# Half of the tokens' merge, output, norm and query moved beside the other half's experts

## The reference

```python
h = rmsnorm(x, g1) * (1 + sc1) + sh1
p = h @ w_in                                    # attention, short convolution, long convolution, gates
g_att, g_sc, g_hy = split(sigmoid(p[..., GT0:]), 3)
m = g_att * (y_att @ w_att) + g_sc * (y_sc @ w_sc) + g_hy * (y_hy @ w_hy)
x = x + gt1 * (m @ w_o)                         # the merge and the output projection
h2 = rmsnorm(x, g2) * (1 + sc2) + sh2
# experts: for each token 8 heads, each with the 16 best of 128*128 experts
q = h2 @ wq;  s = q . subkeys;  e, score = top 16 of the sums of the top 16 of both halves
a = gelu(u_tab[e] . h2);  f = sum over heads and experts of softmax(score) * a * v_tab[e]
x = x + gt2 * f
```

## Time and profile before

| | us |
|---|---|
| median of three runs | 5394.02 |
| lowest, highest | 5386.65, 5394.62 |
| span of the profiled execution (first to last instruction) | 5406.6 |
| busy in it: PE matmul | 3763.2 (70%) |
| PE weight load | 1823.9 (34%) |
| VectorE | 3264.4 (60%) |
| ScalarE | 1947.0 (36%) |
| GpSimd | 1959.6 (36%) |
| DMA, all queues | 1532.43 MB, mean 283 GB/s |

### The profile page before, as it was taken

How to read it: one execution, slowest core, us unless ns; L and a number is a source line. 1 busy time by engine, 2 the same in 40 slices (tenths; PEclk the granted TensorE clock), 3 DMA queues, 4 the chain that set the end, 5 groups by cost and what they waited for, 6 DMA issues and landing times. The chain is left out here.

```text
span 5406.6 us, 59650 instructions
## 1 busy us (share of the span) xinstructions
PE 3763.2 (70%) x19504; PEld 1823.9 (34%) x19504; DVE 3264.4 (60%) x7012; ACT 1947.0 (36%) x5112; POOL 1959.6 (36%) x1521
## 2 busy tenths in 40 slices
PE   6899879987555555555497788668976555555554
PEld 3677338876111111111122245246852111111111
DVE  7522452323777777777647778764136777777776
ACT  5432002222434334434334434325223433443443
POOL 5112003322444444444343356212433444444443
PEclk7999889998777777777798889889987777777777
DMA  5011001112999999999999989831328999999998
GB/s 238 16 44 71 4 16 63 62 71 89 399 420 410 414 408 421 413 414 415 391 407 358 361 335 378 348 146 42 100 84 334 421 410 416 410 418 416 410 418 347
DMA packets 230644, 1532.43 MB, mean 283 GB/s; under 512 B 26164, under 2 KB 26740, under 8 KB 58044
## 3 DMA queue, kind: packets, MB, share of 16 engines
q0 software_dynamic: 184320, 1342.26, 60.7%
q1 hardware_dynamic: 46012, 186.36, 9.3%
HBM read 1515.31 MB, written 13.21 MB: 283 GB/s over the span
## 5 line engine op out<-in xcount | busy, mean ns | idle before, releaser
L536 PE MATMUL psum<-arena 64*64 64x512 f32 x10240 | 1752.8, 818 | 1230.9 <-ACT arena L515 1207.1
L491 POOL DMA_INDIRECT arena<-in_uv,arena x1280 | 1446.9, 1130 | 1878.1 <-PE psum L536 1438.7
L651 DVE SCALAR_TENSOR_TENSOR arena<-arena 128x1024 f32<-128x1024 f32 x1280 | 1597.5, 1248 | 736.9 <-DMA arena<-in_uv,arena 681.0
L536 PEld LDWEIGHTS psum<-arena 64*64 64x64 f32 x10240 | 415.4, 168 | 2524.9 <-ACT arena L515 1880.4
L1527 PE MATMUL psum<-view_at,view_at 128*128 128x512 f32 (+1 forms) x4896 | 964.7, 358 | 19.3 <-PEq L165 10.3
L504 ACT ACTIVATE arena<-arena 128x1 f32<-128x1 f32 x1280 | 258.3, 202 | 1865.1 <-DVE arena L651 1794.2
L1527 PEld LDWEIGHTS psum<-view_at,view_at 128*128 128x128 f32 x4896 | 813.9, 191 | 183.7 <-issue 53.3
L265 POOL TENSOR_TENSOR view_at<-view_at,view_at 128x1024 fp32r<-128x1024 f32 (+1 forms) x180 | 398.8, 2225 | 1208.7 <-ACT view_at L299 1207.7
L515 ACT ACTIVATE arena<-arena 128x64 f32<-128x64 f32 x1280 | 445.1, 348 | 75.8 <-PE psum L536 33.9
L508 ACT ACTIVATE arena<-arena 128x1 f32<-128x1 f32 x1280 | 376.8, 294 | 47.1 <-ACT arena L504 0.8
L299 ACT ACTIVATE view_at<-view_at 128x1024 fp32r<-128x1024 f32 (+1 forms) x176 | 164.0, 939 | 327.9 <-DMA view_at<-in_w_in 186.4
(11 more groups left out here) (243 smaller groups left out, 3368.4 us busy)
## 6 DMA issues: line engine op xcount, KB each, us to landing
view_at<-in_w_in SPq DMA_DIRECT2D x108, 512.0 KB, 5.6
view_at<-in_w_mod SPq DMA_DIRECT2D x48, 1024.0 KB, 11.6
arena<-in_uv,arena POOLq DMA_INDIRECT x1280
view_at<-in_w_br SPq DMA_DIRECT2D x48, 256.0 KB
view_at<-in_w_out SPq DMA_DIRECT2D x16, 512.0 KB, 8.7
view_at<-in_wq SPq DMA_DIRECT2D x16, 512.0 KB, 3.3
arena<-mod_rows SPq DMA_DIRECT2D x12, 512.0 KB
keep_spectrum<-arena SPq DMA_DIRECT2D x18, 256.0 KB, 7.3
```

The costliest lines, as they stand in the source:

```text
L491: nc.gpsimd.indirect_dma_start(out=self.slots[i % self.ring], out_offset=None, in_=self.table, in_offset=bass.IndirectOffsetOnAxis(ap=self ...
L536: last = nc.tensor.matmul(self.c.psum[tokens, at:at + 512], self.diag[rows, k % 4], self.slots[k % self.ring][rows, D + h * 512:D + (h + 1 ...
L651: nc.vector.scalar_tensor_tensor(out=self.junk, in0=self.slots[i % self.ring][:, 0:D], scalar=1.0, in1=self.h2_turned if i % 2 else self.h ...
```

## The change

Layer 1: merge, out, norm2 and query run on the four latent tiles only. The context's rounded input h and its three branch outputs are stored to DRAM at the start of the merge. The experts then run alone for 260 steps (the phase is given 260, two tiles and 4). The context pair's merge, output, norm and query follow as one phase, `phase_later_beside`, beside the steps 260 to 492, and the experts go on alone to step 520.

Layer 2: the same with the second pair of latent tiles; its phase runs beside the steps 0 to 236 of the first pair.

`phase_later_beside` has a list of steps with weights: a lead, 24 gates and 24 values, the eight blocks of `w_out`, the norm, the eight blocks of `wq`, each 256 tokens wide. All weights are loaded from DRAM a second time, through a ring of three slots that lie where space is left (`ScatteredRing`). The sigmoid is written with tanh, `(tanh(z/2) + 1) * v`, and m is halved when it is rounded. It uses the PSUM banks 0 to 3, so the experts' tiles beside it are on banks 4 to 7: `(4, 0, 4, 0, 4, 4)` becomes `(4, 0, 4, 4, 4, 4)` and `(0, 4, 0, 4)` becomes `(4, 4, 0, 4)`.

```diff
 class Share:
-    def __init__(self, experts=None, first=0, last=0, steps=1):
-        self.experts, self.first, self.n, self.steps = experts, first, last - first, steps
+    def __init__(self, experts=None, first=0, last=0, steps=1, weights=None):
+        self.experts, self.first, self.n = experts, first, last - first
+        self.ends = [0] + list(itertools.accumulate(weights or [1] * steps))
...
+LAST_LATENTS = Later(2, 0, 152, (88, 96), 168, ((176, 180), (189, 193), (197, 132)))
+CONTEXT = Later(4, 1, 168, (96, 80), 136, ((144, 148), (189, 193), (197, 132)))
...
+def later_steps():
+    steps, weights = [("lead", i) for i in range(3)], [4] * 3
+    for g in range(N_GATES):
+        steps += [("gate", 2 * g), ("value", 2 * g + 1)]
+        weights += [4, 2]
+    steps += [("merged", i) for i in range(2)]
+    weights += [1] * 2
+    steps += [("out", N_MERGE + b) for b in range(KD)]
+    weights += [4] * KD
+    steps += [("added", i) for i in range(2)] + [("norm", i) for i in range(6)]
+    weights += [1] * 2 + [2] * 6
+    steps += [("query", N_MERGE + KD + h) for h in range(PH)]
+    weights += [5] * PH
+    steps += [("scored", i) for i in range(2)]
+    weights += [1] * 2
+    return steps, weights
...
+def phase_later_beside(c, layer, where, experts, first, last, h_kept, ys_kept):
...
+        @ph.block.gpsimd
+        def _(pool):
+            for s, (kind, n) in enumerate(steps):
+                share.gpsimd(pool, s)
+                if kind == "lead" and n == 2:
+                    ring.split(pool, 0)
+                if kind in ("gate", "value", "out", "query"):
+                    ring.split(pool, n + 1)
...
+                    feature_job(c, ring.parts(n), bank(n), W, kt, of, after=lambda k: share.tensor(pe, s, k, kt)).then_inc(proj, 1)
...
+                    nc.scalar.activation(sig[:, g % 2], c.psum[:, bank(n - 1):bank(n - 1) + W], ACT.Tanh, scale=0.5).then_inc(sig_d, 1)
...
+                if kind in ("gate", "value", "out", "query"):
+                    ring.round_one(act, n + 2)
...
 def phase_merge
+            ring.load(sp, proj, range(SLOTS))
+            for dst, src in stores:
+                sp.dma_start(dst, src).then_inc(stored, 16)
+            ring.load(sp, proj, range(SLOTS, n_all))
...
 def build
-        phase_merge(c, 0, lay)
-        phase_out(c, 0, True, lay)
-        phase_norm2(c, 0, True)
-        experts = Experts(c, 0, range(NT), (4, 0, 4, 0, 4, 4))
-        phase_query(c, 0, True, experts)
+        phase_merge(c, 0, lay, NT_LAT, [(h_kept, c.hT[:, :, later])] + [(ys_kept[br], lay.ys[br][:, :, later]) for br in range(3)])
+        phase_out(c, 0, lay, NT_LAT)
+        phase_norm2(c, 0, NT_LAT)
+        experts = Experts(c, 0, range(NT), (4, 0, 4, 4, 4, 4))
+        phase_query(c, 0, NT_LAT, experts)
+        group = GROUP_TILES * experts.per_tile
+        phase_experts(c, experts, group + 4)
+        phase_later_beside(c, 0, CONTEXT, experts, group + 4, 2 * group - 20, [h_kept], ys_kept)
...
-        phase_merge(c, 1, lay)
-        phase_out(c, 1, False, lay)
-        phase_norm2(c, 1, False)
-        experts = Experts(c, 1, range(NT_LAT), (0, 4, 0, 4))
-        phase_query(c, 1, False, experts)
+        phase_merge(c, 1, lay, GROUP_TILES, [(kept, h.bitcast(F32)[:, :, later]) for kept, h in zip(h_kept, (lay.hT_high, lay.hT_low))]
+                    + [(ys_kept[br], lay.ys[br][:, :, later]) for br in range(3)])
+        phase_out(c, 1, lay, GROUP_TILES)
+        phase_norm2(c, 1, GROUP_TILES)
+        experts = Experts(c, 1, range(NT_LAT), (4, 4, 0, 4))
+        phase_query(c, 1, GROUP_TILES, experts)
+        phase_later_beside(c, 1, LAST_LATENTS, experts, 0, group - 20, h_kept, ys_kept)
         phase_experts(c, experts, experts.n_all)
```

More of the change, by code:

```diff
@@ L36 @@
 NT = NT_LAT + NT_CTX
+GROUP_TILES = 2
+GROUP_W = GROUP_TILES * P
 GRID_W = 64
@@ L283, in __init__, with load @@
         self.high_ready, self.ready = ph.sem("w_high_ready"), ph.sem("w_split")
-    def load(self, sp, used):
-        for n in range(self.ahead, len(self.blocks)):
+    def load(self, sp, used, blocks=None):
+        for n in range(self.ahead, len(self.blocks)) if blocks is None else blocks:
             block, kt = self.blocks[n]
@@ L333, in parts, with __init__, load, round_one @@
         return self.high[:, n % self.slots], self.low[:, n % self.slots]
+class ScatteredRing:
+    def __init__(self, c, ph, blocks, places):
+        self.c, self.blocks, self.slots = c, blocks, len(places)
+        self.raw = [c.own(raw, KD, P) for raw, _ in places]
+        self.low = [c.rounded(raw, KD, P) for raw, _ in places]
+        self.high = [c.rounded(high, KD, P) for _, high in places]
+        self.landed = [ph.sem(f"w_landed{s}") for s in range(self.slots)]
+        self.high_ready, self.ready = ph.sem("w_high_ready"), ph.sem("w_split")
+    def load(self, sp, n, used):
+        block, kt = self.blocks[n]
+        if n >= self.slots:
+            sp.wait_ge(used, n - self.slots + 1)
+        sp.dma_start(self.raw[n % self.slots][:, 0:kt], block).then_inc(self.landed[n % self.slots], 16)
+    def round_one(self, act, n):
+        if n < len(self.blocks):
+            s, kt = n % self.slots, self.blocks[n][1]
+            act.wait_ge(self.landed[s], 16 * (n // self.slots + 1))
+            self.c.nc.scalar.activation(self.high[s][:, 0:kt], self.raw[s][:, 0:kt], ACT.Copy).then_inc(self.high_ready, 1)
+    def split(self, pool, n):
+        if n < len(self.blocks):
+            s, kt = n % self.slots, self.blocks[n][1]
+            pool.wait_ge(self.high_ready, n + 1)
+            split(self.c.nc, self.c.nc.gpsimd, self.high[s][:, 0:kt], self.low[s][:, 0:kt],
+                  self.raw[s][:, 0:kt]).then_inc(self.ready, 1)
+    def wait(self, pe, n):
+        pe.wait_ge(self.ready, n + 1)
+    def parts(self, n):
+        return self.high[n % self.slots], self.low[n % self.slots]
 class Mixing:
@@ L1519, in feature_job @@
     nc = c.nc
-    for lo, hi in ((0, 512), (512, width)):
+    for lo, hi in ((0, min(512, width)), (512, width)):
         if hi <= lo:
@@ L2294, in norm_rows, with phase_merge @@
     return [c.at(140, D), c.at(148, D)], [c.at(144, D), c.at(112, D)]
-def phase_merge(c, layer, lay):
+def phase_merge(c, layer, lay, nt, stores):
     nc, io = c.nc, c.io
-    width = lay.tokens
+    width = nt * P
     ys, y_high, y_low = lay.ys, lay.y_high, lay.y_low
@@ L2313, in phase_merge @@
         ring = SplitRing(c, ph, blocks)
-        proj, sig_d, gated, steps, h_rounded, h_split, y_rounded, y_split = (ph.sem(s) for s in (
-            "projected", "sigmoid_done", "gated", "dve_steps", "h_high_ready", "h_split", "y_high_ready", "y_split"))
+        proj, sig_d, gated, steps, h_rounded, h_split, y_rounded, y_split, stored = (ph.sem(s) for s in (
+            "projected", "sigmoid_done", "gated", "dve_steps", "h_high_ready", "h_split", "y_high_ready", "y_split", "later_stored"))
         @ph.block.sync
         def _(sp):
-            ring.load(sp, proj)
+            ring.load(sp, proj, range(SLOTS))
+            for dst, src in stores:
+                sp.dma_start(dst, src).then_inc(stored, 16)
+            ring.load(sp, proj, range(SLOTS, n_all))
+            if stores:
+                sp.wait_ge(stored, 16 * len(stores))
         @ph.block.gpsimd
@@ L2386, in _, with phase_out @@
                     st.do(nc.vector.tensor_tensor(mT[:, i, 0:width], mT[:, i, 0:width], dst, ALU.add))
-def phase_out(c, layer, full, lay):
+def phase_out(c, layer, lay, nt):
     nc, io = c.nc, c.io
-    T = lay.tokens
+    T = nt * P
     mT, m_low, m_high = c.own(lay.mT_at, KD, T), c.rounded(lay.mT_at, KD, T), c.rounded(lay.m_high_at, KD, T)
@@ L2471, in query_blocks, with phase_norm2 @@
     return [(c.io["wq"][layer][h], KD) for h in range(PH)]
-def phase_norm2(c, layer, full):
+def phase_norm2(c, layer, nt):
     nc = c.nc
-    tiles = list(range(NT if full else NT_LAT))
+    tiles = list(range(nt))
     h2N = c.at(80, NT, D)
@@ L2489, in _ @@
             ring.load(sp, None)
-            for s in range(2 if full else 1):
-                sp.dma_start(c.at(128 + 4 * s, D), spread_row(c, layer, GT2, s)).then_inc(gate_in, 16)
-            sp.wait_ge(gate_in, 32 if full else 16)
+            sp.dma_start(c.at(128, D), spread_row(c, layer, GT2, 0)).then_inc(gate_in, 16)
+            sp.wait_ge(gate_in, 16)
         @ph.block.gpsimd
@@ L2537, in _, with phase_query @@
                 last.then_inc(turned, 1)
-def phase_query(c, layer, full, experts):
+def phase_query(c, layer, nt, experts):
     nc, io = c.nc, c.io
-    width = T_ALL if full else L_LAT
-    nt = width // P
+    width = nt * P
     qTs = [c.at(at, T_ALL) for at in (104, 107, 110, 113, 116, 194, 197, 200)]
```

299 lines of the change are left out of this document (292 added, 7 removed).

## The result

The changed kernel takes 5300.11 us (median of four runs, 5291.74 to 5309.56) against 5393.45 us of the kernel before on the same chip (four runs, 5386.65 to 5394.62): a ratio of 0.9829, 95% interval 0.9814 to 0.9843, or 92 us less by the ratio. The forecast was 5339 us, 55 us less, with a range of 5278 to 5425. The sign and the mechanism held; the price of the work that was moved was forecast too high.

A forecast was written before the change was run, and what follows sets the result against it. PE bounds up to the first gather, the DMA engines after it. Terms -162.5 - 121 + 206 + 13 + 9 = -55.5 us on the 5406.6 us span give 5351, or 5339 us for the median; range 5278 to 5425.

The forecast's parts named there:

- Serial half of layer 1: Layer 1's merge, out, norm2 and query on 512 tokens in place of 768: 162.5 us less.
- Serial half of layer 2: Layer 2's merge to first gather at width 256 in place of 512: 121 us less (bounds 100 and 140).
- The ring: Layer 2's merge: weight slots come round late, PE waits for GpSimd's split, 4.9 us a gate against PE's 4.3.
- The stores: Start of layer 2's merge: 3.7 MB of stores delay the load of block 4, 5 us (bounds 0 and 10).
- The bytes: Stages beside the experts: reloaded weights and kept parts, 32 and 33 MB; with bubbles 102 + 104 = 206 us more.
- the bubbles: Stages beside the experts: DMA engines at 97% of the pure rate, 691 and 703 us.
- Seams and banks: Experts' stages: three more phase ends draining gathers, 13 us; three more tile changes sharing PSUM banks, 9 us.
- Rival 1: Stages beside: GpSimd's gathers queue behind weight splits, 375 GB/s; 33 us slower, 5427 us; chance 0.17.
- Rival 2: Stages beside: DMA queue never empty, 670 and 682 us; 109 us less, 5284 us; chance 0.20.
- the likeliest case: Whole change as stated with bubbles of about 3%: 5339 us, own range 5305 to 5375; chance 0.52.
- Rival 3: Layer 2's serial half doesn't shrink, by PE's clock or an 8 us gate: 80 us come back, 5419; chance 0.06.
- Rival 4: Stages beside: tanh and gelu switch ScalarE tables, 62 us a pair; +123 us if none hidden, 5462; chance 0.05.

The follow-up runs named there:

- the three bare seams: Kernel before, nothing moved, its experts' phases ended at steps 260, 492 and 520 of layer 1 and 236 of layer 2: 5402.94 us, ratio 1.0012.
- the run with the banks alone: Kernel before with only the experts' PSUM banks set as in the changed kernel: 5393.17 us, ratio 1.0001.
- the run with layer 2 alone: Kernel before with the change made in layer 2 only, layer 1 still on 768 tokens: 5387.07 us, ratio 0.9966.
- six slots: Changed kernel with six weight ring slots in place of four in layer 2's merge: 5285.45 us, ratio 0.9773; with stores in pieces too, 5282.84 us, 0.9776.

## Why the prediction was right or wrong

**Serial half of layer 1: right.** From the first matmul to phase_out 199.7 us (forecast 199.9, from layer 2's rows), then 142.0 (142.7). The first gather stands at 1173.2, forecast 1172. Rows of another layer with the same shape were worth more than any sum of parts.

**Serial half of layer 2: right mechanism, 9 us too hopeful.** The ring binds, as forecast: PE waits for GpSimd's split, 3.39 us at the third gate and 12.7 us over the 21 gates after it, 0.6 a gate, which is the forecast's number. Yet two gates take 10.2 to 10.4 us where 9.7 were forecast, and the merge takes 130.3 us against 125. Two terms of the round were too small. From a load's issue to the end of its split go 7.1 us here and 6.8 in the kernel before (medians of 20 loads; the landing is the part that grew), in a merge where the DMA share is 0.49 and not 0.27. And after a wait PE takes 3.17 us for a block's 24 matmuls (3729.75 to 3732.92), where the forecast had 2.88. The clock adds to it:

```profile
3651.00:3657.00 6.00, 4.35 (x20) 4.38 (x21) 2.50 (x1) 3.81 (x4) 6.00 (x4) 0.50 1.08 386
3668.00:3671.00 3.00, 3.00 (x16) 3.00 (x16) 2.35 (x1) 0.61 (x1) 3.00 (x3) 0.51 0.02 5
```

The granted clock is 0.50 in the merge's first 4 to 5 us, and again 0.51 in 3668 to 3671, behind the 3.39 us in which PE stood idle. The stores were put at 5 us; cut in pieces they give at most 2, but no run leaves them out. From phase_out to the first gather 42.2 us went where 23, 3 and 20 were forecast.

**The bytes: right, and the bubbles weren't there.** From gather 260 to gather 492 the stage takes 682.2 us and before 586.8: 95.4 more, where 102 were forecast; in layer 2 (the first 236 steps) 689.7 against 594.3: again 95.4, where 104 were. The step that failed is the one that read the rate off the convolution stage. There the DMA share was 0.96 at 375 GB/s, and I took 97% of the pure rate, a third of the way towards it. The trace has a share of 1.00 at 405 and 406 GB/s. The rate is lower than the gathers' own because the weights' packets move 385 GB/s in their share, not because engines stand idle: 243 MB of gathers at 412 and 32 MB at 385 are 674 us of layer 1's 682, and some 4 of the other 8 are the dips in its two seam windows. What made the convolution's stage slower stood in my own text, PE's 3.0 us a step and its stores, and GpSimd's 64.0 us of waits; in the new stage the last is 6.7. The average loads, on the other hand, came out as worked: DVE 80% (forecast 80), ACT 46 (47), POOL 63 (62), PE 72 (70 to 92).

**Seams and banks: too dear.** 6.5 in place of 13 and 0 in place of 9. A seam's dip was priced as lost time from one window; the three bare seams lose 6.1, 2.6 and 1.4 us of DMA time and cost half of the forecast, and in the changed kernel they lose 6 us of DMA time in all. Bank sharing was priced from what PE waits, though the end that binds is the gathers'; in the run with the banks alone PE's waits for VectorE's add in layer 2's experts go from none to 11.0 us in two waits, but the 24 gathers around that tile change (step 128) take 61.3 us against 60.1 in the kernel before, and those around layer 1's step 384 61.7 against 64.7. The gathers don't pay for PE's wait.

**What the table shows beyond that.** Of layer 1's 84.0 us, 95.4 are the stage, and some 9 come back at its start: the first eight gathers take 27.7 us in the profile of before and 18.6 after. The runs with seams or banks alone have the old code there and took 20.3 and 20.4, the run with layer 2 alone 26.8, and the runs with the new code 18.6 to 21.6, so a good part of it can be the scatter of one profiled execution, and so, by the same comparison, are the mixed stages' -5.4: the code is the same, and the runs here have 1043 to 1053 us. That fits the 98.9 us of the spans being some 6 or 7 more than the runs' (93 by the medians, 92 by the ratio).

**The rivals.** Rival 1 needed 383 GB/s or less; the stage never came near it. Rival 2, no bubbles, 5284 us, is nearer to the measured 5300 than the likeliest case, and its mechanism is the one in the trace, a DMA share of 1.00. Its stage times of 670 and 682 us stand against 682 and 690. So the total came into the range by errors that partly cancel: the experts' parts were priced at 228 us more and took 180 more in the table above, and the serial half of layer 2 was 9 us too hopeful. Rival 2 had a chance of 0.20 where the row for it (406 GB/s beside the modulation) deserved more weight. Rival 3 is out: the clock in layer 2's merge is 0.97, and its stretches at the lower level are 8 us long, which cost 4 us by estimate and not 80. Rival 4 is out by the table loads. The Trainium skill's page "ScalarE: Activation LUTs", section "Table sets: the hidden batching unit", puts tanh beside exp and sigmoid. No load stands before the 24 tanh between gelus, so here gelu's set holds tanh as well, and the measurement decides.

## What to carry to other kernels

Work moved from a stage bound by PE under one bound by DMA costs its bytes and little more (95 us here for 32 MB that take 83 at the 385 GB/s of their queue); but look at the next bound too, since taking the bytes away gave back only half of their time until GpSimd's splits went as well. Halving the width of a stage that streams weights moves its bound from PE to the ring: price the round of a slot (landing, rounding, split), and give the ring slots. To price a new mixed stage from an existing one, ask first what slowed the existing one (here GpSimd's 64.0 us of waits, which the new stage doesn't have).

## What the runs showed of the hardware

- Tanh runs with gelu's table in place: 24 tanh among 219 gelus, no load. Sigmoid needs one each way: 46 loads more, 1283 ns each.
- A 128 x 1024 dot on VectorE takes 1227 ns alone and 1440 to 1457 ns where GpSimd subtracts 64 blocks in 230 steps; without the subtractions 1242 (the last two with few weight bytes).
- Three products or one: with the DMA engines at a share of 1.00, 58 us less of PE's busy time in 640 changed nothing.
- A 128 x 128 by 256 matmul stream with its own weight load each runs at 0.120 us a matmul when fed: with six slots 864 of them take 107.5 us from the first to the last, waits included. After a wait of 0.3 us, 24 of them took 3.17 us and not 2.88.
- Gathers of 8 KB rows and loads of weight blocks share the 16 DMA engines with no idle time between them: 410 and 385 GB/s in their own shares of 88.0% and 11.6%.
